# Memory attention with its query norm applied per token, as the scale of the exponential, and not spread over the queries

## The reference

```
def rmsnorm(x, g):
    y = x * rsqrt(mean(x * x, axis=-1, keepdims=True) + EPS)
    return y * g

q = rmsnorm((h @ w_q).reshape(B, S, XA_HEADS, XA_HEAD_DIM), g_q)
k = rmsnorm(kv[:, :, 0], g_k)
s = einsum('bshd,bmhd->bhsm', q, k) * (XA_HEAD_DIM ** -0.5)
p = softmax(s, axis=-1)
out = einsum('bhsm,bmhd->bshd', p, v)
```

## Time and profile before

| | before |
|---|---|
| time, median of 3 runs | 1576.63 us (1574.66 to 1583.11) |
| the profiled execution | 1582.68 us, span 1581.2 us |
| TensorE busy | 1431.4 us, 91% of the span |
| VectorE, ScalarE, GpSimd busy | 999.4, 822.4, 82.8 us |
| mean granted TensorE clock | 0.946 of full speed |

### The profile page before, as it was taken

One profiled execution on the slowest core, in us unless ns is written; L12 is line 12 of the kernel. 1 busy time (PEld: TensorE's weight loads), 2 busy tenths in 40 slices (PEclk: granted clock), 3 DMA queues, 4 the chain that ended last, 5 costly groups with the idle time before them and its releaser, 6 DMA issues.

```text
span 1581.2 us, 18449 instructions
## 1 busy us (share of the span) xinstructions
PE 1431.4 (91%) x7139; PEld 1188.1 (75%) x7139; DVE 999.4 (63%) x755; ACT 822.4 (52%) x712; POOL 82.8 (5%) x93
## 2 busy tenths in 40 slices
PE   5998887999989998877999999999999999999994
PEld 4987465878869987465778878788778788777883
DVE  4456333454354372333688887888877888878885
ACT  4424123433344432222667676676767767667772
POOL 2020100000000020001000000000000000000001
PEclk9999978999998987887999999999999999999997
DMA  9412313545496320402999989989899899998997
GB/s 296 134 63 98 113 67 131 202 143 184 146 311 226 115 81 27 179 1 87 340 353 349 359 323 393 342 348 371 320 385 359 330 375 346 363 350 331 376 360 262
DMA packets 115563, 392.96 MB, mean 249 GB/s; under 512 B 7892, under 2 KB 45376, under 8 KB 115520
## 3 DMA queue, kind: packets, MB, share of 16 engines
q1 hardware_dynamic: 103344, 370.85, 63.2%
q0 software_dynamic: 3456, 12.58, 2.2%
q10 hardware_dynamic: 8720, 8.91, 1.6%
HBM read 376.07 MB, written 16.25 MB: 248 GB/s over the span
## 4 chain that ended last, share of the span: by engine, by line
PE 72%; DVE 15%; ACT 6%; issue 5%; POOL 1%; SPq 1%; DMA 1%; DVEq 0%; POOLq 0%; ACTq 0%
PE bank L1339 35%; PE bank L1335 17%; PE bank L1336 16%; DVE wl L945 10%; ACT wh L673 4%; PE bank L1725 1%; PE bank L1347 1%; PE bank L1632 1%; ACT aT L702 1%; DVE scratch L1075 1%; DVE scratch L1058 0%; DVE xn L928 0%; PE bank L1436 0%; ACT xn L663 0%; PE bank L1510 0%
## 5 line engine op out<-in xcount | busy, mean ns | idle before, releaser
L945 DVE TENSOR_TENSOR wl<-ring,wh 128x2816 fp32r<-128x2816 f32 (+2 forms) x245 | 755.8, 3096 | 250.3 <-ACT wh L673 235.0
L673 ACT ACTIVATE wh<-ring 128x2816 fp32r<-128x2816 f32 (+2 forms) x245 | 622.8, 2542 | 351.1 <-PE bank L1336 299.3
L1335 PE MATMUL bank<-wh,xh 128*128 128x512 f32 (+1 forms) x960 | 367.4, 383 | 30.4 <-DVE wl L945 22.3
L1336 PE MATMUL bank<-wh,xl 128*128 128x512 f32 (+1 forms) x960 | 362.2, 377 | 0.0
L1335 PEld LDWEIGHTS bank<-wh,xh 128*128 128x128 f32 x960 | 181.8, 189 | 78.2 <-issue 30.5
L1339 PE MATMUL bank<-wl,xh 128*128 128x512 f32 (+1 forms) x960 | 238.1, 375 | 0.0
L1336 PEld LDWEIGHTS bank<-wh,xl 128*128 128x128 f32 x960 | 181.9, 189 | 27.1
L1339 PEld LDWEIGHTS bank<-wl,xh 128*128 128x128 f32 x960 | 176.9, 188 | 23.7
L1335 PE MATMUL bank<-wh,ah 128*128 128x512 f32 x440 | 174.9, 397 | 6.1 <-DVE wl L945 5.4
L1336 PE MATMUL bank<-wh,al 128*128 128x512 f32 x440 | 171.7, 390 | 0.0
L1339 PE MATMUL bank<-aT,wh 128*128 128x256 f32 x448 | 112.3, 287 | 4.2 <-DVE aT_low L968 2.1
(11 more groups left out here) (226 smaller groups left out, 1130.2 us busy)
## 6 DMA issues: line engine op xcount, KB each, us to landing
ring<-in_we_gate SPq DMA_DIRECT2D x66, 1408.0 KB, 7.3
ring<-in_we_up SPq DMA_DIRECT2D x66, 1408.0 KB, 8.1
ring<-in_we_down SPq DMA_DIRECT2D x56, 1536.0 KB, 8.7
ring<-in_w_in SPq DMA_DIRECT2D x16, 1536.0 KB, 8.0
ring<-in_w_gate SPq DMA_DIRECT2D x8, 1408.0 KB, 6.1
ring<-in_w_up SPq DMA_DIRECT2D x8, 1408.0 KB, 6.1
ring<-in_w_down SPq DMA_DIRECT2D x6, 1536.0 KB, 6.6
rows_of<-zeros ACTq DMA_DIRECT2D x1, 8704.0 KB, 37.0
```

The lines of the kernel that those rows point to most:

```text
L673: nc.scalar.activation(wh[:, j, 0:n], ring[:, slot, 0:n], ACT.Copy).then_inc(high_ready, 1)
L945: nc.vector.tensor_tensor(wl[:, j, 0:n], ring[:, slot, 0:n], wh[:, j, 0:n].bitcast(F32), ALU.subtract).then_inc(low_ready, 1)
L1335: nc.tensor.matmul(dst, x_high, w_high, start=first, stop=False)
L1336: return nc.tensor.matmul(dst, x_low, w_high, start=False, stop=False)
```

## The change

The queries are multiplied by the gain alone, and the factor of the norm is applied after the scores, where a token is a partition: the scale of the exponential is now the tensor `xqr` (one column for each head and half), and the negated maximum is multiplied by the same column. `xqr` is (128 * (mean square + EPS)) ** -0.5, so the factor 128 ** -0.5 of the scores is in it. The means come from 8 matmuls with the squares as the weights and one column of `selh` as the moving operand, into 8 columns of a new bank use `xqm`; GpSimd computes the power. `ssxq`, `bxq0` and `bxq1` go, and with them the logarithm, the first value, its refinement and the spreading. The squares are now taken by ScalarE from the banks `xq0` and `xq1`, one instruction for each, after VectorE has read the bank. The scores of heads 0 and 1 are computed ahead of the means, those of heads 2 and 3 behind them.

```
-    names += [f"yT{i}" for i in range(4)] + ["xq0", "xq1", "ssxq", "bxq0", "bxq1"]
-    names += [f"xs{h}" for h in range(4)] + [f"xpt{h}" for h in range(4)] + ["xo0", "xo1"]
+    names += [f"yT{i}" for i in range(4)] + ["xq0", "xq1"]
+    names += ["xs0", "xs1", "xqm", "xs2", "xs3"] + [f"xpt{h}" for h in range(4)] + ["xo0", "xo1"]
...
 (GpSimd)
+                pool.wait_ge(xq_mean, l + 1)
+                nc.gpsimd.tensor_tensor(xqr[:], xqr[:], neghalf[:].unsqueeze(2).to_broadcast([P, XH, 2]), ALU.pow).then_inc(xq_rstd, 1)
...
 (ScalarE)
-                    act.wait_ge(*taken(l, f"xq{i}"))
-                square(l, "xq", sq[:, 0:4, :], zqk[:, 0:4, :])
-                guess_rows(l, "xq", "ssxq", mxq[:])
+                    act.wait_ge(*full(l, f"xq{i}"))
+                    act.wait_ge(xq_gained, 2 * l + i + 1)
+                    nc.scalar.activation(sq[:, 2 * i:2 * i + 2, :].rearrange("p a s -> p (a s)"), bank(l, f"xq{i}")[:], ACT.Square
+                                         ).then_inc(take(l, f"xq{i}"), 1)
...
-                                                   bias=xnm[:, h, q:q + 1], scale=XHD ** -0.5,
+                                                   bias=xnm[:, h, q:q + 1], scale=xqr[:, h, q:q + 1],
...
 (VectorE)
-                    nc.vector.tensor_copy(zqk[:, 2 * i:2 * i + 2, :].rearrange("p a s -> p (a s)"), bank(l, f"xq{i}")[:]
-                                          ).then_inc(take(l, f"xq{i}"), 1)
-                refine_rows(l, "xq", "ssxq", mxq[:])
-                for i in range(2):
-                    dve.wait_ge(*full(l, f"bxq{i}"))
-                    qq = zqk[:, 2 * i:2 * i + 2, :].rearrange("p a s -> p (a s)")
-                    nc.vector.scalar_tensor_tensor(qq, qq, col(l, "xq"), bank(l, f"bxq{i}")[:], ALU.mult, ALU.mult
-                                                   ).then_inc(take(l, f"bxq{i}"), 1)
+                    nc.vector.tensor_scalar(zqk[:, 2 * i:2 * i + 2, :].rearrange("p a s -> p (a s)"), bank(l, f"xq{i}")[:],
+                                            col(l, "xq"), None, ALU.mult).then_inc(xq_gained, 1)
+                dve.wait_ge(*full(l, "xqm"))
+                nc.vector.tensor_scalar(xqr[:], bank(l, "xqm")[:, 0:2 * XH].rearrange("p (h q) -> p h q", q=2), EPS, float(XHD),
+                                        ALU.add, ALU.mult).then_inc(take(l, "xqm"), 1)
+                dve.wait_ge(*taken(l, "xqm"))
+                nc.vector.engine_nop().then_inc(xq_mean, 1)
                 for h in range(XH):
                     dve.wait_ge(*full(l, f"xs{h}"))
                     then_wait(nc.vector.tensor_reduce(xnm[:, h, :], bank(l, f"xs{h}")[:].rearrange("p (q m) -> p q m", q=2),
                                                       AX_X, ALU.max, negate=True))
-                    nc.vector.tensor_scalar(xnm[:, h, :], xnm[:, h, :], XHD ** -0.5, None, ALU.mult).then_inc(xmax_ready, 1)
+                    if h == 0:
+                        dve.wait_ge(xq_rstd, l + 1)
+                    nc.vector.tensor_tensor(xnm[:, h, :], xnm[:, h, :], xqr[:, h, :], ALU.mult).then_inc(xmax_ready, 1)
...
 (TensorE)
-                pe.wait_ge(squares_ready, SQUARES[l, "xq"])
-                mean_rows(l, "ssxq", selh, 3, 4, sq, XH)
-                pe.wait_ge(rows_ready, ROWS[l, "xq"])
-                spread_rows(l, "bxq", spreadh[:], mxq[:], XH)
                 for i in range(2):
                     pe.wait_ge(*taken(l, f"bmk{i}"))
+                def memory_scores(*heads):
+                    for h in heads:
+                        ps = open_bank(l, f"xs{h}")
+                        pe.wait_ge(xq_gained, 2 * l + h // 2 + 1)
+                        for q in range(2):
+                            ins = mm(ps[:, q * S:q * S + S], zqk[:, h, q * P:q * P + P], xk[:, h, :], True, True)
+                        ins.then_inc(done(l, f"xs{h}"), 1)
+                memory_scores(0, 1)
+                for i in range(2):
+                    pe.wait_ge(*taken(l, f"xq{i}"))
+                ps = open_bank(l, "xqm")
                 for h in range(XH):
-                    ps = open_bank(l, f"xs{h}")
-                    pe.wait_ge(*taken(l, f"bxq{h // 2}"))
                     for q in range(2):
-                        ins = mm(ps[:, q * S:q * S + S], zqk[:, h, q * P:q * P + P], xk[:, h, :], True, True)
-                    ins.then_inc(done(l, f"xs{h}"), 1)
+                        ins = mm(ps[:, 2 * h + q:2 * h + q + 1], sq[:, h, q * P:q * P + P], selh[:, 3:4], True, True)
+                ins.then_inc(done(l, "xqm"), 1)
+                memory_scores(2, 3)
```

More of the change, by code:

```diff
@@ L287, in build @@
         mmk = sb("mmk", [4, S])
-        mxq = mmk
+        xqr = sb("xqr", [P, XH, 2])
         newton = sb("newton", [16, S])
@@ L353, in build @@
         xmax_ready = sem("xmax_ready")
+        xq_gained = sem("xq_gained")
+        xq_mean = sem("xq_mean")
+        xq_rstd = sem("xq_rstd")
         xprobs_ready = sem("xprobs_ready")
@@ L382, in build @@
                 RSTDS[l, n] = len(RSTDS) + 1
-            for n in ["qk0", "qk1", "qk2", "qk3", "mk", "cv", "fox", "xq"]:
+            for n in ["qk0", "qk1", "qk2", "qk3", "mk", "cv", "fox"]:
                 SQUARES[l, n] = len(SQUARES) + 1
-            for n in ["qk", "cv", "mk", "xq"]:
+            for n in ["qk", "cv", "mk"]:
                 ROWS[l, n] = len(ROWS) + 1
```

## The result

| | before | after |
|---|---|---|
| time, median of 4 runs each | 1575.64 us (1570.32 to 1583.11) | 1557.15 us (1551.69 to 1559.51) |
| ratio of the times | | 0.9844 (95% interval 0.9806 to 0.9883) |
| the profiled execution | 1582.68 us, span 1581.2 us | 1551.69 us, span 1550.2 us |
| mean granted TensorE clock | 0.946 | 0.959 |

The change makes the kernel faster by 1.6%, with an interval from 1.2 to 1.9%. The ratio on record is not that of the two medians: those differ by 18.5 us, which is 1.2% and lies at the near end of the interval. The two spans differ by 31.0 us.

The account below looks back on a forecast made before the run. The prediction took the chain from last query matmul to last maximum as latency the whole kernel waits for; 9.84 + 10.60 - 2 x 0.5 = 19.4 us off the median 1576.63 gave 1557.2 us, range 1550 to 1566.

Parts of the forecast that it names:

- What bounds the kernel: Last query matmul to last maximum in cross-attention: latency the whole kernel waits for, 17.49 us in layer 0, 18.25 in layer 1.
- Scores of heads 0 and 1: TensorE right after the last query matmul: 8 records in 1.72 us, covering gain multiply and square with 0.3 to spare.
- Means, 1.71 us: TensorE's 8 mean matmuls behind the first scores: 16 records in 1.71 us, 3.42 at half clock.
- Power, 1.67 us between 0.72 and 2.93: GpSimd's power of eight columns, on the path: 1.67 us, growing by 0.158 a column.
- Rival (c): GpSimd's power costs as much for eight columns as for two: 1.9 us more gained, 1555.3 us; chance 0.08.
- Maxima 0.96 apart: VectorE's maxima of the four heads after the power: one head takes 0.96 us.
- Table load of 1.28 us in layer 1: Extra link of layer 1's old chain, ahead of the exponential: 1.28 us, gone with the change.
- Clock behind the maxima: TensorE partly at half clock after a longer stillness: 0.5 us lost a layer, bounds 0.7 gain to 3.4 loss.
- Rival (a): Half clock for all the values' matmuls, 3.4 us a layer, and part of the means: 1561 to 1565 us; chance 0.15.
- (b): Half clock holds on TensorE through the projection: 34.7 us lost against 20.4 gained, 1591 us, slower; chance 0.02.
- The gain carried through to the end unchanged: After both cross-attentions, TensorE sets the pace, so their whole gain, 19.4 us, reaches the kernel's end.
- Rival (d): Layer 0's lead is lost in the dense mixer or layer 1's weights: only 10.1 us gained, 1566.5 us; chance 0.05.

Follow-up runs that it names:

- e1_means_first: The changed kernel with the means ahead of all scores on TensorE; median 1562.83 us, ratio 0.9897.
- e10_before_filled: The kernel before, with TensorE's idle time in the norm's chain filled by added matmuls whose results are overwritten; ratio 0.9972.
- e4_power_16: The changed kernel with GpSimd's power taken over 16 columns instead of 8, the other 8 unused; one run, 1567.71 us.
- e3_no_norm: The changed kernel without the query norm's factor: no squares, means or power, the scale is the constant alone; median 1544.86 us, ratio 0.9782.
- e5_fill_gap: The changed kernel with 8 matmuls filling TensorE's stillness between the last score and the first transposition; median 1557.6 us, ratio 0.9847.
- e8_split_and_fill: The changed kernel with the power in two instructions of 4 columns and TensorE's stillness filled with 7 matmuls; median 1555.22 us, ratio 0.9831.
- e6_tables_back: The changed kernel with a logarithm and an exponential on constants, and both table loads, put back on ScalarE in layer 1; one run, 1552.5 us.
- e7_immediate_scale: The changed kernel with a constant as the exponential's scale, the norm's factor computed and not used; one run, 1557.12 us.

## Why the prediction was right, and where not

*What bounds the kernel.* Right. The stretch was open latency. In layer 1 its 11.0 us appear in the stage, less the 0.5 that the clock took behind it (10.43). In layer 0 only 8.15 of the 10.25 appear: 0.7 went behind it and 1.4 ahead of it. From the mark to the last query matmul the first profile of before took 19.18 us, the changed kernel 20.57. The other two profiles of before have 20.38 and 20.46 there, and a stretch of 15.55. The mean granted clock says the same: 0.91 ahead of the stretch and 0.61 in it in the first profile, 0.75 and 0.78 in the other two. So in the profile that the prediction was read from, this layer had more of its half clock inside the stretch, and 9.84 us is what the edit gives against that profile; against the other two it is 8.3.

*Scores of heads 0 and 1, 1.72 us, covering gain multiply and square.* Right: 8 records from 210.42 to the start of the means at 212.16 are 1.74. The gain multiply took 0.75 (forecast 0.70), and the square's end came 1.49 after the last query matmul, the means from 1.58, so 0.09 was left of "0.3 to spare". `e1_means_first` shows that the scores cover a wait that exists anyway: without them the means start after 1.74.

*Means, 1.71 us.* Right. 16 records from 212.16 to 214.08 are 1.92 by the model of their ends, the next scores start 1.78 after the first of them, and the power starts 3.84 after the last query matmul, where the forecast has 3.80.

*Power, 1.67 us between 0.72 and 2.93.* Right: 1.636, 1.008 for four columns, 2.894 for sixteen. Rival (c), eight columns as cheap as two, is refuted: the measured slope is 0.157 us a column. The Trainium skill (GPSIMD Engine Reference, section 3.1, Elementwise) has its 2.6 cycles an element from an addition of two inputs; these traces show that the figure does not carry over to a power.

*Maxima 0.96 apart.* Mis-sized, 0.80 measured. I took 230.88 to 231.84 as VectorE's own pace, and the second of these maxima started 0.03 after TensorE's last scores ended (221.65 + 10.16), so it had waited for them. In the changed kernel nothing is waited for between them:

```profile
216.24 0.68 DVE L1144 TENSOR_REDUCE xnm<-bank 128x2 f32<-128x512 f32 x1
...
217.03 0.69 DVE L1144 TENSOR_REDUCE xnm<-bank 128x2 f32<-128x512 f32 x1
...
217.83 0.68 DVE L1144 TENSOR_REDUCE xnm<-bank 128x2 f32<-128x512 f32 x1
```

The second maximum came 5.66 after the last query matmul (forecast 5.73), and two intervals of 0.16 less make up the rest of the 0.4 us by which the stretch is shorter than the 7.65 forecast.

*Second tensor operand of the exponential, hidden.* Right: 0.084 us measured, 0.085 forecast, no effect on the stage.

*Table load of 1.28 us in layer 1.* Right, and sharper than forecast: put back, it costs nothing.

*Clock behind the maxima, 0.5 us a layer.* Right for the first pair of profiles: from the last maximum to the last residual addition 23.67 - 22.95 = 0.72 and 23.54 - 23.05 = 0.49. The other two profiles of before have 22.3 in layer 0, so it is 1.3 there against them, while their stretches are 15.55 and not 17.50, again for the clock. The stage in layer 0 differs by 8.2 us in the first pair and by 7.4 on average. Rival (a) took the right cause and put it at 3.4 us a layer, several times too high; (b) did not come near: the clock was at 1.00 from 225.10 on, through the projection.

*The gain carried through to the end unchanged.* This is the step that failed. The sum 19.4 us covers the two cross-attentions. They give 7.4 + 10.45 = 17.9 on average over three profiles each, and layer 1's mixer, of which the forecast said nothing, 188.72 - 182.06 = 6.7 more. The profiles thus put the gain at 24.5 us, and so do the pairs with equal length of layer 0's mixer. With 24.5 us of some 1580 the ratio would be 0.9845, and 0.9844 was measured. The medians gained only 18.5 in that comparison and 19.45 in the next, as the runs of each kernel happened to fall among the lengths of the unedited parts. So the forecast gain was too small by about a fifth by the profiles, and that the predicted 1557.2 met a median of 1557.15 is luck: the draw of runs gave the difference back. Rival (d), layer 0's lead lost on the way, was wrong in sign; its 1566.5 lay just outside the range that was said to take in most of it.

Open: what in the 215 us of layer 0's dense part hands the clock over in one of a few positions. Four kernels (before, `e10_before_filled`, `e1_means_first`, `e4_power_16`) have 188.6 to 188.9 in layer 1's mixer, three (`e3_no_norm`, `e5_fill_gap`, `e8_split_and_fill`) 184.6 to 184.8, and three (the changed one, `e6_tables_back`, `e7_immediate_scale`) 182.0 to 182.1. The three in the middle also have the shortest dense part, 214.3 to 214.4 against 214.9 to 215.2; the other two groups do not differ in it. That what runs earlier decides it is argued from this repetition; no experiment shifted that part alone.

## What to carry to other kernels

- A per-token factor on the rows of a product can be applied where tokens are partitions, as the scale of an activation that is there anyway. What it saves is the latency of making and spreading the factor, if nothing covers that; the extra operand costs nothing while another engine sets the pace.
- Price a link of the chain by what waits for it. The same table load was a link of 1.28 us before and cost nothing when put back after; a maximum's spacing in the trace was its supplier's, not its own.
- When a stage gets shorter, profile each kernel more than once and compare unedited stages. One that repeats in every profile of each kernel, but differs between the two kernels, is part of the measured gain and no merit of the edit, and the next edit may give it back, as `e5_fill_gap` and `e8_split_and_fill` gave back 2.5 to 2.7 us of it.

## What the runs showed of the hardware

- A power on GpSimd costs 0.72 us for 2 columns of 128 partitions, 1.01 for 4, 1.64 for 8, 2.89 for 16.
- TensorE's clock fell from its upper to its lower level (2.4 to 1.2 GHz) not only during a stillness of 3.75 us (changed kernel, 215.9 to 219.67), but also in the middle of work with no pause over 0.20 us, after 8 records with four rows of weights (`e10_before_filled`, layer 1); in layer 0 of the same kernel it held. Why it fell in the one and not in the other is open.
- Seven or eight matmuls whose result nobody reads, put into a wait of 3 to 4 us, were repaid by 1.25 to 1.4 us a layer behind the maxima, with no cost in the stretch ahead of them. The kernel's time did not show it, since unedited parts grew by as much or more in those profiles.
